# A two-block transformer on one core: the modulation vectors move out of the first attention, from TensorE to VectorE

## What is computed

```python
x = first_block(x, ...)      # two attentions, w_out, then conv_ffn: up projection, convolution, gelu * value, down projection
mod_x = silu(c) @ w_ada + b_ada            # w_ada is 1024 x 6144
mod_c = silu(c_ctx) @ w_ada + b_ada
sh1, sc1, g1, sh2, sc2, g2 = split(mod_x, 6)
csh1, csc1, cg1, csh2, csc2, cg2 = split(mod_c, 6)
hx = rms_norm(x, norm1) * (1 + sc1) + sh1
hc = rms_norm(ctx, norm1) * (1 + csc1) + csh1      # ... scans, windowed attention on projections of hx and hc
x = x + g1 * (concat(ssd_x, attn_x) @ w_out)
h = rms_norm(x, norm2) * (1 + sc2) + sh2           # ... mixture of 32 experts
x = x + g2 * moe(h)
```

## Time and profile before

| | us |
|---|---|
| median of 3 runs | 1692.51 (1691.05 to 1697.25) |
| the profiled execution | 1692.79 |
| its span | 1690.9 |
| TensorE busy in it | 1470.6 (87%) |
| VectorE busy | 705.5 (42%) |
| ScalarE busy | 500.5 (30%) |
| mean granted clock | 0.941 of full |

### The profile page before, as it was taken

The page is one execution under the profiler, slowest core; times in us unless marked ns, Lnnn a source line. Parts: engine busy times, 40 slices in busy tenths (PEclk is TensorE's granted clock), DMA queues, the critical chain, the costliest instruction groups (busy, mean ns, idle before and its releaser), DMA issues. The chain is left out here.

```text
span 1690.9 us, 19866 instructions
## 1 busy us (share of the span) xinstructions
PE 1470.6 (87%) x7567; PEld 996.8 (59%) x7567; DVE 705.5 (42%) x1363; ACT 500.5 (30%) x911; POOL 131.8 (8%) x196
## 2 busy tenths in 40 slices
PE   6898999799999999989998887956988888878882
PEld 5776565678888878878887776743333333323331
DVE  4744555445555553353564686372111111111114
ACT  4444555443344332242335543330000000000001
POOL 0000000000000000001002213001111111111100
PEclk9899999799999999999999999977999899998996
DMA  7217552024333322213110000463999999999994
GB/s 220 72 49 287 180 186 109 26 75 125 100 97 80 97 85 92 99 27 125 43 58 25 2 1 1 199 248 132 411 405 413 415 407 413 405 404 406 403 400 165
DMA packets 104846, 316.39 MB, mean 187 GB/s; under 512 B 13137, under 2 KB 64689, under 8 KB 90947
## 3 DMA queue, kind: packets, MB, share of 16 engines
q1 hardware_dynamic: 92608, 300.50, 47.3%
q0 software_dynamic: 5760, 12.08, 2.1%
q10 hardware_dynamic: 6403, 2.80, 0.6%
HBM read 311.14 MB, written 12.58 MB: 191 GB/s over the span
## 5 line engine op out<-in xcount | busy, mean ns | idle before, releaser
L1250 PE MATMUL bank<-weights_high,hT_high 128*128 128x512 f32 (+2 forms) x736 | 256.5, 387 | 18.2 <-DVE hT_low_a L1729 4.9
L1250 PE MATMUL bank<-weights_low,hT_high 128*128 128x512 f32 (+2 forms) x560 | 215.4, 385 | 0.0
L1691 DVE TENSOR_TENSOR weights_low<-ring,weights_high 128x2048 fp32r<-128x2048 f32 (+2 forms) x61 | 135.7, 2224 | 186.2 <-ACT weights_high L933 183.9
L933 ACT ACTIVATE weights_high<-ring 128x2048 fp32r<-128x2048 f32 (+2 forms) x61 | 113.3, 1857 | 199.5 <-PE bank L1250 157.2
L1250 PEld LDWEIGHTS bank<-weights_high,hT_high 128*128 128x128 f32 x736 | 141.4, 192 | 47.1 <-issue 9.4
L1250 PE MATMUL bank<-hT_high,weights_high 128*128 128x512 f32 x416 | 166.5, 400 | 1.6 <-DVE hT_low L1729 1.6
L1250 PE MATMUL bank<-hT_low,weights_high 128*128 128x512 f32 x416 | 164.1, 395 | 0.0
L1250 PE MATMUL bank<-hT_high,weights_low 128*128 128x512 f32 x416 | 163.4, 393 | 0.0
L1250 PE MATMUL bank<-ring,hTc 128*64 128x512 f32 (+1 forms) x544 | 134.4, 637 | 32.9 <-DMA ring<-in_w_up 32.9
L1223 ACT ACTIVATE hTc<-bank 128x512 f32<-128x512 f32 x32 | 19.1, 597 | 457.2 <-PE bank L1250 457.2
L2182 DVE TENSOR_TENSOR hT<-hT,bank 128x256 f32<-128x256 f32 x32 | 13.5, 421 | 335.4 <-ACT hT L1227 335.4
(11 more groups left out here) (308 smaller groups left out, 2040.5 us busy)
## 6 DMA issues: line engine op xcount, KB each, us to landing
arena<-in_w_up SPq DMA_DIRECT2D x16, 2048.0 KB, 23.9
arena<-in_w_down SPq DMA_DIRECT2D x16, 2048.0 KB, 23.0
ring<-in_w_gate SPq DMA_DIRECT2D x16, 2048.0 KB, 17.9
ring<-in_w_up SPq DMA_DIRECT2D x16, 2048.0 KB, 23.0
ring<-in_w_down SPq DMA_DIRECT2D x16, 2048.0 KB, 22.2
arena<-in_w_gate SPq DMA_DIRECT2D x15, 2048.0 KB
ring<-in_w_ada SPq DMA_DIRECT2D x12, 2048.0 KB, 9.5
ring<-in_w_up SPq DMA_DIRECT2D x44, 512.0 KB, 5.2
```

The costliest lines, as they stand in the source:

```text
L933: high_ready.tick(s.activation(part_view(w_high, key), raw_view(key), ACT.Copy), k)
L1250: return nc.tensor.matmul(o, lhsT, rhs, start=start, stop=stop)
L1691: low_ready.tick(v.tensor_tensor(part_view(w_low, key), raw_view(key), part_view(w_high, key), ALU.subtract), k)
```

## The change

The attention loop loses the row products, the copies, the sums and the additions. Instead:

- SyncE loads w_ada in 48 parts (m, r), 512 KB each: two of the eight rows j, 512 columns. They go to four stages in `xn`, which is free after the norm before the up projection. Sixteen parts (m 0 to 3, shift and scale of the first norm, for both conditions) are loaded among the w_up units, one per step from f = 2; the other 32 (one condition) among the w_down units, three or four per step from i = 2. A load waits until VectorE has used what lay there.
- VectorE multiplies each row of a part with its value of silu(c), one per partition, and adds to a running sum of 128x512: four instructions per part for two conditions, two for one. The sum over partitions is left.
- TensorE makes this sum with a column of ones: for shifts and scales into 32 partitions (`ada_rows`, at f = 7, 11, 15, 19 and once after w_kvd), for gates into all 128 partitions (after w_kvd).
- ScalarE copies the rows and stores them to DRAM (`mod_rows`), and SyncE loads them back as columns (`columns`), behind the last w_up unit and behind the third w_xbc unit.
- VectorE adds the bias and forms the gains: the first two before the drains of the context norm, the third before the second attention.

The diff, cut to its core:

```diff
+        def early_ada(f):
+            return EARLY_ADA[f - 2:f - 1] if f >= 2 else []
+        def late_ada(i):
+            return [key for k, key in enumerate(LATE_ADA) if 2 + k * (FT // 2 - 2) // len(LATE_ADA) == i]
...
-        for m in range(12):
-            unit(("w_ada", m), f"slot{m % RING}", 512, [(0, wada_v[:, :, m * 512:m * 512 + 512])], ("modrow", m))
...
+        def modulation(sp, parts):
+            for m, r in parts:
+                place = STAGE_AT[m, r][0]
+                older = [key for key in ADA_PARTS[:ADA_PARTS.index((m, r))] if STAGE_AT[key][0] == place]
+                if older:
+                    ada_used.wait(sp, older[-1])
+                elif place == 3:
+                    banks.filled(sp, ("ada", 3))
+                sp.dma_start(ada_stage[place], wada_v[:, 2 * r:2 * r + 2, m * 512:m * 512 + 512]).then_inc(ada_in[place], 16)
+        def columns(sp, first):
+            if first:
+                sp.wait_ge(row_stored, 16 * ROWS_BEFORE[6])
+                for c in range(2):
+                    sp.dma_start(mod[:, c, 0:2, :], h_d[6 * c:6 * c + 2, :].rearrange("s (p j) -> p s j", j=KT)).then_inc(
+                        mod_in, 16)
...
+                if key[0] == "w_up":
+                    modulation(sp, early_ada(key[1]))
+                elif key[0] == "w_down":
+                    modulation(sp, late_ada(key[1]))
+                if key in (("w_up", FT - 1), ("w_xbc", 2)):
+                    columns(sp, key[0] == "w_up")
...
+            def mod_rows(m):
+                bank = banks.filled(act, ("ada", m))
...
+                row_copied.tick(s.activation(mod_row[0:rows, :], bank[0:rows, :], ACT.Copy), m)
+                row_copied.wait(act, m)
+                for n, (part, c) in enumerate(ADA_ROWS[m]):
+                    at = 6 * c + part // 2
+                    act.dma_start(h_d[at:at + 1, (part % 2) * 512:(part % 2) * 512 + 512],
+                                  mod_row[32 * n:32 * n + 1, :]).then_inc(row_stored, 16)
...
-                if q in ROW_AT:
...
-                    for j in range(KT):
-                        quarter = bank[32 * (j % 4):32 * (j % 4) + 32, :]
-                        last = mm(quarter, csilu[:, j, :], w[:, j, :], j < 4, j >= 4)
-                    banks.close(last, ("modrow", m))
...
+            def ada_rows(m):
+                bank = banks.open(pe, ("ada", m))
+                ada_used.wait(pe, (ADA_ROWS[m][-1][0], KT // 2 - 1))
+                for n, (part, c) in enumerate(ADA_ROWS[m]):
+                    last = mm(bank[32 * n:32 * n + 32, :], C("one").broadcast_to([P, 32]), ada_sum(part, c), True, True)
+                banks.close(last, ("ada", m))
...
+            def modulation_sums(parts):
+                for m, r in parts:
+                    place, loaded = STAGE_AT[m, r]
...
+                    dve.wait_ge(ada_in[place], loaded)
+                    for j in range(2):
+                        for c in range(2 if m < 4 else 1):
+                            acc, w, by = ada_sum(m, c), ada_stage[place][:, j, :], csilu[:, c, 2 * r + j:2 * r + j + 1]
+                            if r == j == 0:
+                                ins = v.tensor_scalar(acc, w, by, None, ALU.mult)
+                            else:
+                                ins = v.scalar_tensor_tensor(acc, w, by, acc, ALU.mult, ALU.add)
+                        if j == 0:
+                            link(ins)
+                    ada_used.tick(ins, (m, r))
+                    ada_used.wait(dve, (m, r))
...
+            dve.wait_ge(mod_in, 32)
+            link(v.tensor_tensor(mod[:, :, 0:2, :], mod[:, :, 0:2, :],
+                                 ada_bias[:, 0:2, :].unsqueeze(1).broadcast_to([P, 2, 2, KT]), ALU.add))
...
+                modulation_sums(late_ada(i))
```

More of the change, by code:

```diff
@@ L517, in two_blocks @@
             banks.plan(("kvd", t), (kvd_copied, t))
+        banks.plan(("ada", 6), (row_copied, 6))
+        for m in ADA_GATES:
+            banks.plan(("ada", m), (gate_done, m))
         for t in range(TT):
@@ L1449, in _ @@
                  lambda i: range(4 * i, 4 * i + 4), fresh="norm1_2")
+            ada_rows(6)
+            for m in ADA_GATES:
+                bank = banks.open(pe, ("ada", m))
+                ada_used.wait(pe, (m, KT // 2 - 1))
+                banks.close(mm(bank[:, :], C("one").broadcast_to([P, P]), ada_sum(m, 0), True, True), ("ada", m))
             grow("w_zq", [((name, t), (a, a + 512), token_parts(t)) for name, a in (("q2", 512), ("z", 0)) for t in range(TT)],
@@ L1899, in _ @@
                 kvd_copied.tick(v.tensor_copy(kvd[:, t, :], bank[:, 0:272]), t)
+            for m in ADA_GATES:
+                bank = banks.filled(dve, ("ada", m))
+                row = gates[:, m // 6, (m % 2) * 512:(m % 2) * 512 + 512]
+                gate_done.tick(v.tensor_tensor(row, bank[:, :], row, ALU.add), m)
             kvd_copied.wait(dve, AT - 1)
```

136 lines of the change are left out of this document (65 added, 71 removed).

## The result

| | before | after |
|---|---|---|
| median, us | 1691.78 (1686.94 to 1697.25, 4 runs) | 1645.82 (1642.45 to 1651.55, 4 runs) |
| profiled execution, us | 1692.79 | 1646.59 |
| its span, us | 1690.9 | 1644.8 |
| TensorE, VectorE busy, us | 1470.6, 705.5 | 1429.3, 789.1 |
| mean granted clock | 0.941 | 0.942 |

The ratio is 0.9719 (0.9691 to 0.9746).

A forecast was written before the change was run, and what follows sets the result against it. The prediction took TensorE as the bound in the attention and projections, DMA in the expert loads. Gain 46.9 less 8.0 for sums and 0.7 for drains is 38.2; 1692.8 - 38.2 = 1654.6 us, range 1648 to 1668.

The forecast's parts named there:

- The gain in the attention, 46.9: First attention: modulation work and cold matmuls leave TensorE, 49.1 us less 1.35 at the start and 0.9 at the end.
- column sums and cold matmuls: Attention: eight column sums removed, 16.1 us; matmuls at the lower clock level no longer occur, 4.6 us.
- Row products and gate sums: Attention, TensorE: twelve row products removed, 22.2 us, and four gate sums removed, 3.4 us.
- The sums on TensorE, 8.0: Up projection and behind w_kvd: five new groups of sums at 0.93 us, 4.6, plus four moved gate sums, 3.4.
- The context drains, 0.7: Before the context drains VectorE forms two gains, delaying TensorE's first down matmul by 0.7 us, upper bound 1.5.
- VectorE and the queues at 0: Both projections: VectorE's additions, the part loads and ScalarE's copies are hidden behind TensorE, cost 0.
- second rival: Down projection loses its cover: loads of a step take 12.5 us instead of 10.9, giving back 14; 1669, chance 0.07.
- More is won: Stretches behind the attention also lose a cold start, or sums are cheaper: up to 7 us more, 1648, chance 0.05.
- first rival: Attention: repeated bare steps (without modulation) take 3.7 us instead of 3.37, costing 9 us; 1664, chance 0.11.
- third and fourth: Attention: third, clock falls once in four bare steps, 11 us, 1666, chance 0.08; fourth, lower clock throughout, 1755, chance 0.03.
- slow rival: Attention: the clock stays at the lower level, 100 us of bare steps last 200; 1755, chance 0.03.

The follow-up runs named there:

- no_modulation: The kernel before without the modulation products in the attention (no w_ada loads, row products, copies, sums or bias additions); 1673.3 us.
- no_columns: The kernel before without the eight sums into columns in the attention; 1702.7 us.
- before_moved: The kernel before with csilu declared behind arena and 14 unused columns in its place, so later buffers lie where the change puts them; 1690.0 us (0.9989).
- before_aligned: The kernel before with 14 unused columns (56 bytes a partition) behind the constants; 1693.4 us (1.0001).
- after_shifted: The changed kernel with two unused columns (8 bytes a partition) behind the constants; 1647.3 us (0.9714).
- padded profiles: The changed kernel with 2 unused columns behind the constants and 240 behind csilu, every buffer at its address before the change; 1650.3 us (0.9758), again 1654.0 (0.9761).
- sums_short: The changed kernel with about half of VectorE's weighted additions left out (68 of 128 stay); 1686.5 us.

## Why the prediction was wrong, step by step

- **The gain in the attention, 46.9: right.** 46.8 us by the traces. Its sum is confirmed by bare steps of 3.37 and by no_modulation (101.9 us from the first score to the last), the part of column sums and cold matmuls by no_columns (19.1 of 19.2). Row products and gate sums were not taken out one by one.
- **The sums on TensorE, 8.0: the mechanism right, some 1.4 us too small.** The up projection of the changed kernel against before_moved, both with the same placement: 241.09 - 236.21 = 4.9 for four groups, where 3.7 was forecast. The term that was put at nothing is the change of operands around a group, 0.4 each time; 0.83 for the group itself is below the 0.93. Behind w_kvd, 4.3 was forecast for group and gates, and the rows show 4.5; the stretch grew by 5.1 in the first pair of traces, by 4.2 in the means of several.
- **The context drains, 0.7: within the bounds.** The stretch from the last tap grew by 0.3 in the first pair of traces, both with a fall of the clock at its start; between two profiles without it (before_aligned 125.4, after_shifted 126.4) it grew by 1.0.
- **VectorE and the queues at 0: right.** An addition takes 0.750 us where 0.7 was taken (bounds 0.68 and 0.81). TensorE has no new wait for it, half of the work left out gains nothing in the up projection, and a w_ada load of 512 KB lands in 4.5 us. The second rival (the down projection loses its cover) is refuted.
- **The step that failed: that unchanged stretches keep their durations.** It is the base of the prediction's sum, 1692.8 - 38.2: only what the change adds or takes moves the time, all else stands at nothing, and a step of the up projection lasts 11.2 us. The diff shrinks `csilu` by 960 bytes a partition, which the prediction did not look at. In the up projection the placement was worth 4.6 us against the profiled before (240.80 against 236.21), 2.3 against the two other profiles of before (238.51), 2.3 to 2.8 in the changed kernel. In whole times it was worth 4 to 7 us in the changed kernel, and 2 in the kernel before, which is no clear difference. A second part is the profile itself: a fall of the clock near 77 us that the changed kernel's profile did not have (-2.9). The dearer sums worked the other way, so the miss of the base was larger than the 9 us suggest.
- **"More is won" named the right side for other reasons.** It expected a cold start lost or cheaper sums. The clock falls behind the attention stayed, and the sums were dearer.
- **The other rivals are refuted.** The repeated bare steps take 3.37 us and not 3.7 (first rival). No record at the lower level lies in the attention of any of the profiles with the change (third and fourth). Also the rule of the Trainium skill (TensorE: Matmul & The Clock Gate, Part 4: PE-mode transpose) that spoke for the slow rival does not show here: 100 us of steps, of which transposes are some 1.3 in 3.37 us, ran at full granted clock.
- **The range.** It reached 7 us below the forecast and the time was 9 below. Both ends were made of events inside the change; the spread of the stretches outside it, some 3 us at the start and 9 in the second attention in single profiles, was in neither.

What stays open: the stages of the padded profiles place only 3 of the 4 to 7 us. And the placement is the smaller part of the miss. In the means of three profiles of before (with before_aligned) and four of the change (with after_shifted), the spans lie 45.8 us apart where 38.2 were forecast. Of these 7.6 us, 1.9 lie in the up projection, where the placement gains 3.1 and the dearer sums cost 1.2; 0.6 lie ahead of the attention, and 4.7 in the second attention (-2.3) and the experts (-2.4), whose instructions are the same and whose spread is as large. Whether the change moves these two at all isn't shown.

## What to carry to other kernels

A diff that changes the size of a buffer changes the address of every buffer behind it, and on an engine that is full this alone can be worth 0.1 to 0.4% (2 us of 1690 here, 4 to 7 of 1650): compare a step of an untouched, saturated stretch in both traces before crediting an edit, and pad the buffers back to tell the two apart. When work is put at a place in an engine's queue, look at what that engine waits for there and what is queued behind it: the same group of sums one step later cost 7.5 us in the up projection (246.2 for 238.7). And where the output decides how much work comes later (tokens to experts), an experiment that leaves values out can only be read by stage.

## What the hardware showed that I had not expected

- The pace of back-to-back matmuls (128x512, rounded f32 halves) depends on where the operands lie: 229 ns with `arena` 960 bytes earlier, without that 231 or 233 ns, varying from run to run, with some steps at 229 in the padded kernel. The down projection, none of whose operands lie behind `csilu`, has 226.7 ns in all seventeen profiles. The Trainium skill (SBUF — State Buffer, SBUF: two separate sides) says that TensorE's reads wait for no other engine; nothing here contradicts that, since VectorE's work halved left the pace as it was (a step of 10.99 us in sums_short). That section says nothing on the address of the operands, which these runs show to count.
- Where the clock falls outside the attention varies from one execution to the next, and a stretch of 215 us of which TensorE is busy for most takes 212 to 222 us by that alone.
- Changing between plain f32 matmuls and rounded ones costs TensorE time beyond the matmuls themselves: 0.4 us around a group of sums and behind the gates, 0.2 in the w_xbc stage (0.42 us to the next start for 0.23, at 886.14 in before).
